# A block on one core: high and low parts for the attention's scores and the sums of squares, another order at the front, and squares on ScalarE

## What is computed

```python
h = rmsnorm(x, norm1_g) * (1.0 + sc1) + sh1        # sh1, sc1, ... from c @ ada_w + ada_b
p = h @ w_in
xr, yr, q, k, v, ga, gb = jnp.split(p, cuts, axis=-1)
xr = causal_dwconv(xr, conv_w, conv_b)
y_a = rg_lru(xr, ...) * jax.nn.gelu(yr)
q = rmsnorm(q per head, q_norm_g);  k = rmsnorm(k per head, k_norm_g)
# per head, 128 rows of q at a time:
z = (q @ k.T) * scale
log_beta = log_sigmoid(z)
log_1mb = where(mask, log_beta - z, 0)
suffix = cumsum(log_1mb, reverse) - log_1mb
y_b = where(mask, exp(log_beta + suffix), 0) @ v
mix = sigmoid(ga) * y_a + sigmoid(gb) * y_b
x = x + gt1 * (mix @ w_out)
h2 = rmsnorm(x, norm2_g) * (1.0 + sc2) + sh2       # then the feed-forward part
```

## Time and profile before

| | us |
|---|---|
| median of 3 runs (lowest, highest) | 2004.26 (2004.02, 2007.66) |
| the profiled execution | 2006.96 |
| its span, first to last instruction | 2004.9 |
| its mean granted TensorE clock | 0.985 |

### The profile page before, as it was taken

How to read it: one execution, slowest core, us unless ns; L and a number is a source line. 1 busy time by engine, 2 the same in 40 slices (tenths; PEclk the granted TensorE clock), 3 DMA queues, 4 the chain that set the end, 5 groups by cost and what they waited for, 6 DMA issues and landing times.

```text
span 2004.9 us, 25312 instructions
## 1 busy us (share of the span) xinstructions
PE 1935.7 (97%) x8720; PEld 1573.5 (78%) x8720; DVE 968.4 (48%) x1140; ACT 907.0 (45%) x1204; POOL 800.4 (40%) x365
## 2 busy tenths in 40 slices
PE   4999999999899999999999999999999999999998
PEld 4777777777688888888888888787777788888887
DVE  6766666666544343222434422346777544434322
ACT  4477777775355554223223222366676322223222
POOL 2233333333244444444444445533332434444443
PEclk9999999999899999999999999999999999999998
DMA  7333333333122222232232233222221222223231
GB/s 287 105 115 126 123 119 118 121 116 126 53 94 102 97 94 94 98 101 85 96 101 96 94 105 105 84 84 74 84 73 64 74 84 94 94 98 101 95 105 73
DMA packets 54471, 203.15 MB, mean 101 GB/s; under 512 B 6048, under 2 KB 6176, under 8 KB 53280
## 3 DMA queue, kind: packets, MB, share of 16 engines
q1 hardware_dynamic: 54432, 202.62, 29.5%
HBM read 200.50 MB, written 2.10 MB: 101 GB/s over the span
## 4 chain that ended last, share of the span: by engine, by line
PE 85%; DVE 7%; ACT 5%; issue 2%; DMA 1%; ACTq 0%; POOL 0%; POOLq 0%; DVEq 0%; SPq 0%
PE bank L612 24%; PE bank L613 24%; PE bank L617 24%; PE bank L963 1%; PE bank L965 1%; PE bank L964 1%; DVE PARTS L1751 1%; DVE TG L1565 1%; PE bank L761 1%; PE bank L996 1%; PE bank L725 1%; DVE MIX L1565 1%; PE bank L753 1%; ACT ARENA L1238 1%; ACT WH L1113 1%
## 5 line engine op out<-in xcount | busy, mean ns | idle before, releaser
L506 POOL TENSOR_TENSOR WL<-ring,WH 128x1024 fp32r<-128x1024 f32 (+2 forms) x326 | 777.7, 2386 | 1150.1 <-ACT WH L1113 1150.1
L1113 ACT ACTIVATE WH<-ring 128x1024 fp32r<-128x1024 f32 (+2 forms) x326 | 338.9, 1042 | 868.8 <-PE bank L617 775.8
L612 PE MATMUL bank<-HH,WL 128*128 128x512 f32 x1744 | 690.0, 396 | 7.1 <-POOL WL L506 3.8
L613 PE MATMUL bank<-HH,WH 128*128 128x512 f32 x1744 | 684.6, 393 | 0.0
L617 PE MATMUL bank<-HL,WH 128*128 128x512 f32 x1744 | 431.7, 389 | 0.5 <-DVE HL L1565 0.5
L612 PEld LDWEIGHTS bank<-HH,WL 128*128 128x128 f32 x1744 | 331.2, 190 | 77.2 <-POOL WL L506 5.2
L613 PEld LDWEIGHTS bank<-HH,WH 128*128 128x128 f32 x1744 | 330.9, 190 | 68.0
L617 PEld LDWEIGHTS bank<-HL,WH 128*128 128x128 f32 x1744 | 327.4, 188 | 69.5 <-DVE HL L1565 1.7
L613 PE MATMUL bank<-FH,WH 128*128 128x512 f32 x544 | 211.6, 389 | 0.0
L612 PE MATMUL bank<-FH,WL 128*128 128x512 f32 x544 | 211.6, 389 | 0.0
L617 PE MATMUL bank<-FL,WH 128*128 128x512 f32 x544 | 135.0, 389 | 0.0
(11 more groups left out here) (324 smaller groups left out, 2099.8 us busy)
## 6 DMA issues: line engine op xcount, KB each, us to landing
ring<-in_stream SPq DMA_DIRECT2D x355, 512.0 KB, 3.3
ARENA<-in_ada SPq DMA_DIRECT2D x8, 1024.0 KB, 13.5
ring<-in_stream SPq DMA_DIRECT2D x8, 448.0 KB, 10.6
XT<-in_xt SPq DMA_DIRECT2D x1, 2048.0 KB, 7.9
result<-XT SPq DMA_DIRECT2D x3, 512.0 KB, 2.7
result<-XT SPq DMA_DIRECT2D x2, 256.0 KB, 2.1
vec<-in_vec SPq DMA_DIRECT2D x1, 220.0 KB, 2.5
```

What stands on the lines that cost most here:

```text
L506: nc.gpsimd.tensor_tensor(WL[:, slot, 0:cols], ring[:, u % RING, 0:cols], WH[:, slot, 0:cols].bitcast(F32), ALU.subtract).then_inc(w_low, 1)
L612: mm(out_ap, part(WL, base, loc, k), xh(k), start=(start and k == 0), stop=False)
L613: mm(out_ap, part(WH, base, loc, k), xh(k), start=False, stop=False)
L1113: A(WH[:, split_at(base, loc)[1], 0:cols], ring[:, u % RING, 0:cols], ACT.Copy).then_inc(w_high, 1)
```

## The change

1. **Front.** x comes in two DMAs, and the squares of its first half begin with the first. VectorE makes the front's eight low weight parts (`first_low`) instead of GpSimd. The last of the eight rows of ada_w in a group is multiplied by c on TensorE (four more one-column float32 matmuls in `first_columns`), so VectorE has six rows instead of seven. VectorE multiplies x by the inverse root before the gain is there (`first_normed`); ScalarE applies gain and shift, once for HH and once in place, and VectorE subtracts. The columns stand after all fourteen matmuls of an odd tile, not in their midst.
2. **Heads, parts.** The squares of q and k get a high part (ScalarE's Square, now rounded) and a low part (VectorE multiplies q by itself and subtracts: `squares_low`, four instructions per head); TensorE sums them in two fp32r matmuls each. q and k get high parts by ScalarE (`normed_high`) and low parts by VectorE (`normed_low`); `scores` has three fp32r matmuls in place of each float32 one.
3. **Heads, order of p.** PH is made right after the gates' sigmoids, ahead of the next unit's high part; tanh and decay come later (`decays`).
4. **Squares at the end of w_out** are made by ScalarE into MIX; VectorE only adds, all but the last, and TensorE sums SS and the last square, two tiles instead of three.

```diff
@@ heads, TensorE
             def q_square(n):
-                pe.wait_ge(q["q_evac"], 2 * n + 2)
-                mm(bank[5][:, :], ones[:, :], M["QSQ"], start=True, stop=True).then_inc(q["q_ms"], 1)
+                pe.wait_ge(signs, 2)
+                pe.wait_ge(q["q_evac"], 4 * n + 4)
+                mm(bank[5][:, :], negones_r[:, :], M["QSH"], start=True, stop=False)
+                mm(bank[5][:, :], negones_r[:, :], M["QSL"], start=False, stop=True).then_inc(q["q_ms"], 1)
...
-                    mm(seg_bank((2, 3, 4), i), M["KN"][:, i * P:(i + 1) * P], M["QN"][:, i * P:S],
-                       start=(i != 3), stop=False, skip_group_check=True)
+                    for n, (kp, qp) in enumerate((("KL", "QH"), ("KH", "QH"), ("KH", "QL"))):
+                        mm(seg_bank((2, 3, 4), i), M[kp][:, i * P:(i + 1) * P], M[qp][:, i * P:S],
+                           start=(i != 3 and n == 0), stop=False, skip_group_check=True)
@@ heads, ScalarE
+            def normed_high(h):
+                act.wait_ge(q["qn_done"], 3 * h + 1)
+                A(M["QH"], M["QN"], ACT.Copy).then_inc(q["qn_done"], 1)
+                act.wait_ge(q["kn_done"], 3 * h + 1)
+                A(M["KH"], M["KN"], ACT.Copy).then_inc(q["kn_done"], 1)
...
             with act.Fori(0, HEADS - 1) as h:
+                normed_high(h)
                 finished(Q)
@@ heads, VectorE
+            def normed_low(n):
+                for done, low_part, x, high_part in (("qn_done", "QL", "QN", "QH"), ("kn_done", "KL", "KN", "KH")):
+                    dve.wait_ge(q[done], 3 * n + 2)
+                    TT(M[low_part], M[x], M[high_part].bitcast(F32), ALU.subtract).then_inc(q[done], 1)
...
                 ada_rows(h, U_HEAD, h, HEAD_UNITS)
+                squares_low(h + 1)
                 log_sum(h)
...
                 q_norm(h + 1)
                 k_norm(h + 1)
+                normed_low(h + 1)
@@ front, TensorE
                 for j in range(4):
+                    mm(to(j), group_rows(p, KD - 1)[:, j * P:(j + 1) * P], v("c", KD - 1),
+                       start=(j == 0), stop=False, skip_group_check=True)
+                pe.wait_ge(first_sum, FIRST_SUMS * (p + 1))
@@ end of w_out, ScalarE
+            def square(m):
+                act.wait_ge(res_done, 8 + m + 1)
+                A(tile_of(MIX, m), tile_of(XT, m), ACT.Square).then_inc(sq_done, 1)
@@ end of w_out, VectorE
-                TT(SQ[:, :], x, x, ALU.mult).then_inc(sq_done, 1)
-                TT(SS[:, :], SS[:, :], SQ[:, :], ALU.add).then_inc(ss_done, 1)
+                for k in {2: (1,), 3: (2,), 4: (3,), 5: (4,), 6: (5, 6)}.get(m, ()):
+                    dve.wait_ge(sq_done, SQ_BEFORE[1] + k + 1)
+                    TT(SS[:, :], tile_of(MIX, 0) if k == 1 else SS[:, :], tile_of(MIX, k), ALU.add).then_inc(ss_done, 1)
```

More of the change, by code:

```diff
@@ L181, in program @@
             PARTS = mixers.enter_context(nc.sbuf_tensor("PARTS", [P, 2 * TRI], F32R))
+        with ExitStack() as rounded:
+            ARENA_R = rounded.enter_context(nc.sbuf_tensor("ARENA_R", [P, ARENA_COLS], F32R))
         with ExitStack() as normed:
@@ L400, in _ @@
             sp.dma_start(vec[:, :], vec_in).then_inc(vec_in_s, 16)
-            sp.dma_start(XT[:, :], xt_in).then_inc(x_in_s, 16)
+            for half, x_s in ((slice(0, KD * S // 2), x_in_s), (slice(KD * S // 2, KD * S), x_second_s)):
+                sp.dma_start(XT[:, half], xt_in[:, half]).then_inc(x_s, 16)
             def first_group(p):
@@ L527, in lows @@
                                             ALU.subtract).then_inc(pool_low, 1)
-            for k in range(KD):
-                split(U_FIRST, k, k, cols=FIRST_COLS)
+            pool.wait_ge(w_low, KD)
             with pool.Fori(0, HEADS - 1) as h:
@@ L1185, in _ @@
                 h_of(2 * p)
+                if p:
+                    first_high(2 * p + 1)
                 h_of(2 * p + 1)
@@ L1340, in _ @@
             weight_high(U_LAST, O7)
+            def square(m):
+                act.wait_ge(res_done, 8 + m + 1)
+                A(tile_of(MIX, m), tile_of(XT, m), ACT.Square).then_inc(sq_done, 1)
+            for m in range(6):
+                square(m)
             out1_finished(O6)
             weight_high(U_UP1, 0)
+            square(6)
+            square(7)
+            norm(1, eps1)
             out1_finished(O7)
             weight_high(U_UP1, 1)
-            norm(1, eps1)
             high(1, 24)
@@ L1728, in _ @@
             k_norm(0)
+            normed_low(0)
             conv_low(0)
```

154 lines of the change are left out of this document (92 added, 62 removed).

## The result

| | before | after |
|---|---|---|
| median of 4 runs (lowest, highest), us | 2004.14 (2003.27, 2007.66) | 1988.43 (1987.43, 1991.17) |
| the profiled execution, us | 2006.96 | 1987.69 |
| its span, us | 2004.9 | 1986.0 |
| mean granted TensorE clock | 0.985 | 0.988 |

The ratio is 0.9921, 95% interval 0.9903 to 0.9938: 15.7 us faster, where 10.9 were forecast. 1988.43 lies in the predicted range. By the traces TensorE comes to the feed-forward part's first matmul 15.84 us earlier (505.98 for 521.82 in the earlier trace rows), which agrees with the difference of the medians. The spans differ by 18.9; the other 3 us lie in code that is not changed, where matmuls run at half speed for a while in either trace (0.43 us from start to start instead of 0.23) and not at the same places. They say nothing of the change.

The account below looks back on a forecast made before the run. TensorE, busy for 97% of the span, was taken as the bound. -3.6 + 4.3 - 3.3 + 0.9 - 9.2 = -10.9 us, from 2004.26 to 1993.4 us; range 1986 to 2001.

Parts of the forecast that it names:

- Front: Front up to its last tile: first projection 5.2 us earlier, part given back by the cycle behind; -3.6 us (-2.7 to -4.6).
- First head: First head: added VectorE work delays V, less the saved wait for PL; +4.3 us (+3 to +5.5).
- The term of 4.8: First head: six added VectorE instructions of 0.7 us plus links ahead of the rows of ada_w delay V by 4.8 us.
- Turns: Turns 2 to 7: each 50.7 us instead of 51.2, -0.55 us a turn, -3.3 in six.
- PH waits 1.4 us there: Turns: ScalarE's sigmoids end at 157.0 us, p is done at 158.35, so PH waits 1.4 us.
- A wait for XR's split: Heads, sign of being wrong: a row of ada_w holds GpSimd's split back 0.25 us, 1.5 us in six turns.
- End of w_out: From w_out's last matmul to the first feed-forward matmul: some 7.5 us, not 17; -9.2 us (-8 to -10).
- the last head: Last head: q and k instructions delay the mix's low parts by 1.45 us, scores give back 0.57; +0.9 us.
- The heads give all they can: Rival, heads: rows miss one split, p is on time, each of six turns gains 1.5 us; 1987.7 us, chance 0.2.
- The front gives nothing: Rival, front: slower clock behind TensorE's waits in each group takes away the -3.6 us; 1997.0 us, chance 0.15.
- The slower one: Rival, heads: TensorE's wait at the products with v drops the clock, 3.3 us a turn; 2013 us, chance 0.07.
- a granted clock below 1 within the heads: Heads: a sign that would show the prediction wrong, TensorE's granted clock falling below 1 there.

Follow-up runs that it names:

- rows_first: The changed kernel with the first head's first four rows of ada_w ahead of that head's other VectorE work: 1983.30 us, ratio 0.9900.
- rows_ahead: As rows_first, with every further head's first four rows of ada_w ahead of the low parts of q and k: 1977.57 us, ratio 0.9859.
- squares_late: The changed kernel with the four VectorE instructions for the squares' low parts behind p's sum and PL: 2022.74 us, ratio 1.0089.
- before_p_order: The kernel before with only the new order of p (PH ahead of the next high part, tanh and decay behind it): 2000.31 us, ratio 0.9968.
- front_low_pool: The changed kernel with the front's eight low weight parts on GpSimd again: 1997.43 us, ratio 0.9960.

## Why the prediction was right, point by point

**Sign and range** held, and so did the mechanism at the front, in the first head and at the end of w_out. In the turns it held only in part, and that their sum came out near is partly luck. The likeliest sum was 4.9 us too small. By its own steps:

- *Front, -3.6 forecast, -5.15 measured.* The first projection was 0.66 us earlier than forecast: the column records began at 18.32 us, not 18.9, and the first eight took 1.71 us, not 1.87. And the cycle behind it gave back 0.70 us, not 1.6: I had put the step at the middle between a hand schedule (0.6) and columns without cover (2.5), and this trace is at the hand schedule. In rows_first, with the same front, it was 1.9 us (67.93 - 23.24 = 44.69 for 42.79), where a stretch at half clock came later, so one trace doesn't decide between the two. That the front is worth this only with both the row and the low parts moved (5.0 and 7.2 us at the first squares) was not seen.
- *First head, +4.3 forecast, +2.78 measured.* The cause was right: V's weights behind VectorE's work, as rows_first proves. The term of 4.8 was mis-sized: six instructions took 4.04 us, 2.65 for the four and 1.39 for the two, since a start that doesn't depend on the one before comes 0.61 us behind it, not 0.69, and a dependent one 0.72. Counted from the last tile, V's projection starts 34.95 us behind it for 31.26, 3.69 later. The wait for PL gave back 0.82 and not 0.5, V's projection the last 0.09. What the sum left out: the wait of 2.0 us at the squares and both stretches at 1.2 GHz. The one at the squares ended before V's weights came and cost nothing here; the one behind V's wait is in both kernels and cancels.

```profile
72.15 0.68 DVE L1782 TENSOR_TENSOR ARENA<-ARENA 128x512 f32<-128x512 f32 x1
...
74.80 0.54 DVE L1757 TENSOR_SCALAR ARENA<-ARENA,vec 128x512 f32<-128x512 f32 x1
...
85.72 0.69 DVE L1776 TENSOR_TENSOR MH<-QKV,MH 128x512 fp32r<-128x512 f32 x1
...
87.11 0.68 DVE L1765 TENSOR_TENSOR PARTS<-ARENA,PARTS 128x512 fp32r<-128x512 f32 x1
...
97.95 1.06 ACT L1139 ACTIVATE WH<-ring 128x1024 fp32r<-128x1024 f32 x1 [5.62 <-DMA ring<-in_stream]
```

- *Turns, -0.55 each forecast, -0.76 measured.* Near in size, for a reason that was only half there. VectorE's schedule came as worked out (p done 31.0 us after the squares; forecast 158.35 - 127.1 = 31.25), and the wait at v came at 0.7 (forecast 0.95). But the step "PH waits 1.4 us there" failed (it waited 0 to 0.20 us), because ScalarE was itself late: the 1.4 us by which the rows of ada_w begin later delayed V's weights, for which ScalarE waited 0.84 to 1.36, a path that I had used for the first head and not followed in the turns. Of the three savings the squares were right, 0.78 (forecast 0.8); PL was worth 0.83 to 0.88 (0.5), and the scores 0.25 and next to nothing in the turn (0.57). And the sum counts the parts' savings toward the turn, where only the order of p changed it. My line of 0.227 us per 512 columns holds for 512 only: in the changed kernel three products took 0.70 us at 512 columns, but 0.61 at 384, 0.44 at 256 and 0.37 at 128, start to start.

```profile
144.16 0.42 PE L751 MATMUL bank<-MH 128*128 128x384 f32 x1
144.42 0.51 PE L751 MATMUL bank<-MH,ML 128*128 128x384 f32 x2
144.77 0.23 PE L754 MATMUL bank<-strictb,identb 128*128 128x128 bf16 x1
144.81 0.31 PE L751 MATMUL bank<-MH 128*128 128x128 f32 x1
144.95 0.39 PE L751 MATMUL bank<-MH,ML 128*128 128x128 f32 x2
145.18 0.23 PE L754 MATMUL bank<-strictb,identb 128*128 128x128 bf16 x1
```

- *The splits.* I had rows 5 and 7 of ada_w stopped; it was row 6, and then a low part of the squares at 149.94 (2.79 us), which comes to the same. The lock's other direction, from the page SBUF — State Buffer (section "SBUF: two separate sides") of the Trainium skill, did reach TensorE at XR. In the second turn it is hardly seen: the split began at 144.76, 0.17 us before the row of ada_w that began at 144.18 ended (0.75 us long), and took 2.42 us. But in the six turns such a row ran on for 0.17 to 0.44 us and the split took 2.42 to 2.70 us, where it took 2.39 in every turn of rows_ahead, which has no row there, and TensorE began XR 0.05 us behind the split's end each time. That is 0.13 us a turn, 0.8 in six, about half of the 1.5 that I had left to the range; only one of the six is long enough to be listed (0.18 us). A wait for XR's split was one of my signs of being wrong. Where PL ran for 0.5 us beside a split, that one took 2.76. So the trace agrees with the rule.

```profile
147.24 0.50 PE L625 MATMUL bank<-HH,WL 128*128 128x512 f32 x1
...
157.33 1.49 DVE L1829 TENSOR_TENSOR PARTS<-ARENA,PARTS 128x1280 fp32r<-128x1280 f32 x1 [0.47 <-ACT PARTS L1280]
...
158.32 2.76 POOL L520 TENSOR_TENSOR WL<-ring,WH 128x1024 fp32r<-128x1024 f32 x1 [6.13 <-ACT WH L1139]
```

- *End of w_out, -9.2 forecast, -9.55 measured, and the last head, +0.9 and +0.62.* The end came as worked out, step by step (below). In the last head two errors offset each other: the scores gave 0.25 and not 0.57, so the delay was near 0.9 and not 1.45.

```profile
498.44 0.39 PE L848 MATMUL bank<-HL,ML 128*128 128x512 f32 x1
498.67 0.95 PE L661 MATMUL bank<-ones,SS 128*128 128x1 f32 x8
500.33 1.05 PE L661 MATMUL bank<-ones,MIX 128*128 128x1 f32 x8 [0.72 <-ACT MIX L1380]
502.21 2.08 PE L649 MATMUL bank<-ident,RS 128*128 128x128 f32 x8 [0.83 <-DVE RS L1628]
505.98 0.77 PE L625 MATMUL bank<-HH,WL 128*128 128x512 f32 x1 [1.69 <-ACT HH L1155]
```

- *Rivals.* "The heads give all they can" was half right: a turn can be 1.72 us shorter (rows_ahead), but not with the rows of ada_w behind the low parts. "The front gives nothing" fell. The slower one did not come at v, and squares_late shows from which side it would. Its sign, a granted clock below 1 within the heads, was there in the first head, behind a wait that the kernel before has too.

## What to carry to other kernels

Before pricing an instruction that is added to an engine with idle time, list everything that it stands ahead of, also the buffers that the engine releases: here two subtractions delayed p, which I had followed, and a weight transfer and through it another engine's list, which I had not, and they cost more than they saved on TensorE. Price short matmuls by rows of their own width, and count a wait in the midst of pipelined work at more than the idle time that the trace names. When a part of a change is judged, ask whether the engine it speeds up arrives at something that starts by another engine's schedule (XR's split); if so it is worth little until that moves. And run each part alone before calling the sum of their savings a gain: here one part, the order of p, made all of it in the turns.

## What the runs showed of the hardware

- The wait of TensorE that the trace calls 0.52 us costs 0.83 (before and before_p_order).
- Behind waits of 3.6 us at v the granted clock was 0.62 over 4.5 us, so partly at 1.2 GHz instead of 2.4, and 2.15 us of products took 3.84; with waits of 0.7 us at the same place the clock stayed at 1.00 from 126 to 430 us. Behind the wait of 3.54 us in the first head it was 0.51 over 3.5 us, and V's projection took 7.20 us instead of 5.44.
- A GpSimd split that starts while a VectorE row still runs takes longer: 2.42 us with 0.17 us of overlap, 2.70 with 0.44, 2.39 with none.
- In the front the clock falls for a few microseconds at a place that differs between executions of equal code: near 48 us in the changed kernel (0.91 on average between 40 and 60 us), near 60 us in rows_first and rows_ahead (1.00 between 40 and 60). That moves what is behind it by up to 1.5 us (first squares at 73.4 to 74.9 us in seven kernels with this front).
- Two VectorE rows beside two GpSimd splits took 3.4 us longer than alone (front_low_pool and the changed kernel).
